# Two products of each column tile widened from 256 to 288 columns, in a two-network transformer kernel on one core

## The reference, cut to what matters

```python
# first_block, layer 0: gating + time mix; layer 1: dilated attention; each followed by
z = h @ w_up                                   # 1024 x 5632
z = conv_w[0] * z2 + conv_w[1] * z1 + conv_w[2] * z + conv_b
x = x + (silu(gate) * val) @ w_down            # 2816 x 1024
...
# second_block, layer 0: attention over one block; layer 1: short convolution; each followed by
g, u = jnp.split(h @ w_gate_up, 2, axis=-1)    # 1024 x 5632
x = x + gate_f * ((silu(g) * u) @ w_down)      # 2816 x 1024
```

## Time and profile before

| what | value |
|---|---|
| median of 3 runs | 1257.17 us |
| the profiled execution | 1257.31 us |
| its span, first to last instruction | 1255.5 us |
| granted TensorE clock, mean | 1.000 |
| TensorE busy | 98% of the span, 9891 products |
| VectorE busy | 75% |
| ScalarE busy | 57% |
| HBM read | 261.17 MB, 209 GB/s over the span |

### The profile page before, as it was taken

How to read it: one execution, slowest core, us unless ns; L and a number is a source line. 1 busy time by engine, 2 the same in 40 slices (tenths; PEclk the granted TensorE clock), 3 DMA queues, 4 the chain that set the end, 5 groups by cost and what they waited for, 6 DMA issues and landing times.

```text
span 1255.5 us, 23514 instructions
## 1 busy us (share of the span) xinstructions
PE 1230.4 (98%) x9891; PEld 1148.8 (92%) x9891; DVE 945.0 (75%) x1279; ACT 719.1 (57%) x1048; POOL 17.4 (1%) x28
## 2 busy tenths in 40 slices
PE   6999999999999999999999999999999999999998
PEld 6989899999999879999988998999998997999997
DVE  4887379888768777999976667899986666677453
ACT  6843477656565677666667457644455554643432
POOL 0112000000000000000000000000000000000000
PEclk9999999999999999999999999999999999999999
DMA  9450287776666265789663544899965356675640
GB/s 323 166 201 4 69 265 238 257 238 211 222 214 251 87 197 206 245 272 312 246 225 115 181 135 134 298 350 351 335 242 201 135 204 198 228 254 189 202 168 34
DMA packets 163875, 263.78 MB, mean 210 GB/s; under 512 B 5869, under 2 KB 98233, under 8 KB 163770
## 3 DMA queue, kind: packets, MB, share of 16 engines
q1 hardware_dynamic: 160586, 259.54, 60.4%
q10 hardware_dynamic: 3184, 2.73, 0.8%
HBM read 261.17 MB, written 1.05 MB: 209 GB/s over the span
## 4 chain that ended last, share of the span: by engine, by line
PE 96%; DVE 1%; ACT 1%; issue 1%; DMA 1%; SPq 0%; ACTq 0%; DVEq 0%
PE ps L1087 25%; PE ps L1058 16%; PE ps L1059 16%; PE ps L1060 16%; PE ps L1073 2%; PE ps L828 2%; PE ps L829 2%; PE ps L827 2%; PE ps L1075 2%; PE ps L1074 2%; PE ps L2336 2%; PE ps L807 1%; DMA ring<-in_ev_w_in_dram 1%; PE ps L2345 1%; PE ps L2536 1%
## 5 line engine op out<-in xcount | busy, mean ns | idle before, releaser
L603 DVE TENSOR_TENSOR wlo<-ring,whi 128x2048 fp32r<-128x2048 f32 x194 | 443.2, 2288 | 95.4 <-ACT whi L597 95.1
L1058 PE MATMUL ps<-ghi,whi 128*128 128x256 f32 x1600 | 448.1, 280 | 0.0
L1059 PE MATMUL ps<-glo,whi 128*128 128x256 f32 x1600 | 447.0, 279 | 0.0
L1060 PE MATMUL ps<-ghi,wlo 128*128 128x256 f32 x1600 | 446.5, 279 | 0.0
L597 ACT ACTIVATE whi<-ring 128x2048 fp32r<-128x2048 f32 x194 | 370.6, 1914 | 84.0 <-PE ps L1087 46.9
L1058 PEld LDWEIGHTS ps<-ghi,whi 128*128 128x128 f32 x1600 | 300.5, 188 | 1.2
L1059 PEld LDWEIGHTS ps<-glo,whi 128*128 128x128 f32 x1600 | 299.9, 187 | 1.2
L1060 PEld LDWEIGHTS ps<-ghi,wlo 128*128 128x128 f32 x1600 | 300.1, 188 | 0.0
L1087 PE MATMUL ps<-whi,yhi 128*128 128x512 f32 x480 | 159.2, 395 | 0.7 <-DVE ylo L1935 0.7
L1087 PE MATMUL ps<-wlo,yhi 128*128 128x512 f32 x480 | 156.7, 390 | 0.0
L1087 PE MATMUL ps<-whi,ylo 128*128 128x512 f32 x480 | 156.6, 390 | 0.0
(11 more groups left out here) (306 smaller groups left out, 1573.2 us busy)
## 6 DMA issues: line engine op xcount, KB each, us to landing
arena<-in_w_ada_dram SPq DMA_DIRECT2D x48, 1024.0 KB, 6.3
ring<-in_ff_w_up_dram SPq DMA_DIRECT2D x44, 1024.0 KB, 7.7
ring<-in_w_gate_up_dram SPq DMA_DIRECT2D x44, 1024.0 KB, 7.2
ring<-in_ff_w_down_dram SPq DMA_DIRECT2D x10, 2048.0 KB, 8.0
ring<-in_w_down_dram SPq DMA_DIRECT2D x10, 2048.0 KB, 8.0
ring<-in_od_w_qkv_dram SPq DMA_DIRECT2D x6, 2048.0 KB, 8.6
ring<-in_w_qkv_dram SPq DMA_DIRECT2D x6, 2048.0 KB, 8.0
ring<-in_w_in_dram SPq DMA_DIRECT2D x6, 2048.0 KB, 8.0
```

Of the source, the lines that this page charges most:

```text
L603: e.tensor_tensor(shaped(WLO[i % NB], k), v, shaped(WHI[i % NB], k).bitcast(F32), ALU.subtract).then_inc(S["w_lo"], 1)
L1058: e.matmul(o, wh, h[0][:, k, :], start=k == 0, stop=False)
L1059: e.matmul(o, wh, h[1][:, k, :], start=False, stop=False)
L1060: x = e.matmul(o, wl, h[0][:, k, :], start=False, stop=k == NK - 1)
```

## The change

In the left half of every column tile, the first of the three products at k = 0 and at k = 4 moves 288 columns in place of 256. The 32 more are the first 32 columns of the next k, since `h[0]` is contiguous over k. Their results land in columns 256 to 287 of the bank, which belong to the right half. The right half's first product has `start=True` and overwrites them. No instruction, wait or transfer is added or taken away.

```diff
+SPILL = 32
...
+        def flat_h(x, k, n):
+            return x.rearrange("p k t -> p (k t)")[:, 256 * k:256 * k + n]
+
         def pe_tile(e, w, key, k_norm, fresh, pair=False, turned=()):
...
                     wh, wl = hi[:, c:c + 128], lo[:, c:c + 128]
-                    e.matmul(o, wh, h[0][:, k, :], start=k == 0, stop=False)
+                    if a == 0 and k in (0, 4):
+                        e.matmul(ps[:, 0:256 + SPILL], wh, flat_h(h[0], k, 256 + SPILL), start=k == 0, stop=False)
+                    else:
+                        e.matmul(o, wh, h[0][:, k, :], start=k == 0, stop=False)
                     e.matmul(o, wh, h[1][:, k, :], start=False, stop=False)
                     x = e.matmul(o, wl, h[0][:, k, :], start=False, stop=k == NK - 1)
```

## The result

The changed kernel takes 1260.74 us (median of 11 runs) against 1256.34 us for the kernel before beside it (11 runs): ratio 1.003, 95% interval 1.0023 to 1.0038. It is slower by 2.9 to 4.8 us. Forecast were 1242 us and a gain.

What follows compares the result with a forecast made beforehand. TensorE's product distances were taken to bound the kernel. 22.0 us gained, less 3.1 for the kicks and 1.3 for failed first kicks, left 17.6; 1257.3 - 17.6 + 2 for VectorE gave 1242 us, range 1237 to 1261.

Steps and rivals of the forecast that it cites:

- What bounds the kernel: TensorE, never out of work (98% of the span); but for some 4% the time is the sum of distances between product starts.
- The two distances: 256-column products run 113.5 or 117.9 ns apart, 4.4 ns different; two self-holding ways for weight loads and products to fall into step.
- Price of 32 columns: At the 218 widened tile products: 14.2 ns each, 3.1 us in all, bounds 2.1 and 10.9 us.
- The lower bound: A widened product inside the long distance has 4.4 ns of slack, so costs 9.8 ns, 2.1 us in all.
- The effect on the products behind it: Behind the kicks, 5001 tile products go to the short distance, 4.4 ns each: 22.0 us gained, the upper bound taken.
- The second kick does little harm: The kick 12 products later does little harm, since the short distance came back after a disturbance in `pe_first`.
- What is late next: VectorE, with slack of 0.43 and 0.64 us in full stages, takes 2 us off the gain, between 0 and 4.
- The first rival: Nothing falls into step, tiles stay long; cost 2.1 to 3.1 us, 1259.4 to 1260.4 us; chance 0.26.
- The slower rival: Each kick unsettles the three or four products behind it, which fall back to the long distance; 7.0 us, 1264; chance 0.12.

Runs made afterwards that it cites:

- the last kernel: Kernel before, 39 products widened: 30 behind 512-column products, 180 in feed-forward 2 and behind modulation, 200 then 216 in long runs; 1244.13 us against 1256.07.
- 763 of them: Against the kernel before, the first product of every k from 0 to 6 in the left half moves 288 columns; 1267.45 us, ratio 1.0091.
- another kernel without a kick: Kernel before with sixteen products widened by 200 columns, in tiles 8, 12, 16 and 20 of each feed-forward; 1251.92 us against 1256.83, ratio 0.996.
- the second profile of the kernel before: The kernel before, unchanged, profiled once more; span 1257.8 us against 1255.5 in its first profile.
- one kick: Changed kernel with only the k = 0 product of each tile widened by 32 columns; 1258.48 us against 1256.43 for the kernel before, ratio 1.0017.
- the narrowed products: Width sweep on the kernel before: a right-half product at k = 4 moves 8 to 128 columns less, left-half ones 8 to 256 more; no time given.

## Why the prediction was wrong, by its own steps

*What bounds the kernel*: right. TensorE is busy but for some 21 us of waits, the same before and after, and its distances add up to the time; every later gain and loss came through them.

*The two distances*: right as a reading, and right that each holds itself. Tiles can be brought from long to short, worth 4.4 ns a product, and the short one holds over halves and tiles (383 products in the last kernel).

*Price of 32 columns*: near. 14.2 ns was taken; measured were 13.7 with 763 of them and 13.8 with 218, or 13.2 with what the products behind give back. The lower bound, that 4.4 ns of the long distance are slack into which columns would fit, was wrong: a widened product in the long run costs its full 13 ns. The Trainium skill's rule that the prediction quotes (TensorE: Matmul & The Clock Gate, Back-to-back issue gap) gives 13.3 ns for the 32 columns, and the traces agree with their 13.2 to 13.8. That there is one distance for 256 columns they don't bear out: there are 113.3 and 117.8 ns.

*The effect on the products behind it*: this is the step that failed. It took the upper bound of 22.0 us, and the measured value for 32 columns is 0: in 109 tiles with 218 kicks not one half came short, and with 763 one did, the right half of the first tile, which came short in another kernel without a kick. I had argued that a kick of 10 to 14 ns is larger than the 3 to 6 ns seen in the earlier trace rows and so would do. Size does not decide. 24 columns (10 ns) take in some places and 30 in others, 32 in none tried, 180, 200 and 216 where smaller ones fail, for the most part by what stood before. The warning was in the rows: in the earlier trace rows late products led straight to the long distance.

*"The second kick does little harm"*: wrong, and it would have cost the gain even with a good width. The earlier trace rows showed one disturbance survived; a kick that takes in the long distance throws out of the short one, seven times of seven. In the changed kernel itself one kick of 288 met the short distance, behind `pe_rows`:

```profile
50.21 0.28 PE L1081 MATMUL ps<-whi,hhi 128*128 128x256 f32 x1
...
50.89 0.29 PE L1064 MATMUL ps<-hhi,whi 128*128 128x288 f32 x1
...
51.14 0.28 PE L1068 MATMUL ps<-hhi,wlo 128*128 128x256 f32 x1
...
51.49 0.28 PE L1068 MATMUL ps<-hhi,wlo 128*128 128x256 f32 x1
```

Six products ahead of it take 0.68 us, 113 ns each, three behind it 0.35, 117 ns each, and the tile stays long; in the second profile of the kernel before, without a kick, the same entry gave two whole tiles at the short distance. The tile of the earlier trace rows is no such case, since `pe_first` ahead of it had gone long by itself.

*What is late next*: right in kind, and less in size. In the changed kernel there was nothing to be late for. The last kernel, with 4216 short products, shows one wait of 1.23 us for VectorE, where 2 us were taken off, in feed-forward 2, which was named.

*The first rival*, that nothing falls into step (0.26), is what happened. Its cost of 3.1 us is the 3.0 measured at the widened products. That 1260.74 lies near its 1260.4 and inside the stated range is partly luck, since the kernel before, timed again beside it, took 1256.34 and not the 1257.3 that the sum starts from.

*The slower rival* had the sign and not the mechanism. Its settling behind each kick isn't there: the three distances behind a 288 lie between 112 and 122 ns, 0.2 ns under the long one on average, and those behind them are at 118. (In about a third of the places a single product comes at 112 or 113 and the next at 118 again: near, and not held.) Of the 3.3 us between the spans 3.0 are columns and 0.5 is `pe_first` coming at the long distance more often, less 0.2 of all else. `pe_first` moves from kernel to kernel (short were 169 of its 672 products before, 279 with one kick, 56 with two) and from one execution to the next (146 in the second profile of before, at other places). The medians are 4.4 us apart, 1.1 more than the spans: the profiled execution of before was 1.0 us above its own median, that of the changed kernel 0.15 below. What made that execution of before longer than most stays open.

One count of the prediction is off: `pe_rows` has twelve runs of 48 in the trace of before, and nine of them are at the short distance, not 7 of 10. Nothing in the sum hangs on it.

What no run here settles is what the two ways of falling into step are, and so why 30 columns take where 32 never did. That it needs equal lengths of a weight load and 256 columns fits the narrowed products and fits the settled 512-column products, which have a single distance, but it was not measured by itself.

## What to carry to other kernels

Where the bounding engine is never idle, read the distances between its instructions' starts: equal instructions at two distances are a reserve that no wait shows. Such a reserve is had by what goes ahead of the run, tried place by place and width by width in one kernel that sweeps them, and kicked once for each run, since a second kick undoes the first. A kick that has not been seen to take is only its own cost. Take a second profile of the unchanged kernel first: which runs are short differs between two executions of one program.

## What the runs showed of the hardware

- A 256-column product with its weight load repeats every 113.3 or every 117.8 ns at the full granted clock, and either goes on for hundreds of products without change (383 short ones in the last kernel, 455 long ones in the kernel before).
- 32 more columns cost 13 ns in the long one; 128 fewer save some 7 ns of two distances (229 ns for 236).
- Which of the two comes is repeatable to a degree I hadn't expected: 30 columns behind a run of 512-column products took in 26 of 26 tiles of two kernels, 200 and then 216 in six of six. It is not fixed: 216 alone took in the second tile of feed-forward 0 in one kernel and failed there in two others, and two executions of the kernel before had 74 and 168 short tile products.
- One execution had the granted clock at 0.50, its lower level, from 72.6 to 74.6 us after its start, with TensorE busy before and in it; 256-column products stood 213 ns apart.
